# One hybrid attention and expert layer on one core: the router taken block by block, a ring of ten weight places, later rounds inside a pair, constant products in waits

## What is computed

```python
xp = xp + gt1 * _rmsnorm(out, g_post1[l])            # out = [conv, attention] @ w_out
h = _modulate(xp, g_pre2[l], sh2, sc2)               # rmsnorm(xp) * g * (1 + sc2) + sh2
xp = xp + gt2 * _rmsnorm(_hier_moe(h, *moe_w), g_post2[l])
...
def _hier_moe(h, w_rg, b_rg, w_re, b_re, w_gate, w_up, w_down):
    g_prob = jax.nn.softmax((xt @ w_rg) + b_rg, axis=-1)
    g_top, g_idx = lax.top_k(g_prob, 1)
    e_logits = ((xt @ w_re) + b_re).reshape(-1, N_GROUPS, E_PER_GROUP)
    e_sel = jnp.take_along_axis(e_logits, g_idx[:, :, None], axis=1)[:, 0]
    e_top, e_idx = lax.top_k(jax.nn.softmax(e_sel, axis=-1), TOP_K)
    ...
    for e in range(N_EXPERTS):                       # 32 experts
        he = jax.nn.silu(xt @ w_gate[e]) * (xt @ w_up[e])
        out = out + gates[:, e:e + 1] * (he @ w_down[e])
```

## Time and profile before

| | us |
|---|---|
| three runs: median, lowest, highest | 729.72, 726.66, 861.23 |
| the profiled execution, its own time | 726.36 |
| its span from first to last instruction | 724.6 |
| PE busy in the span | 589.2 (81%) |
| DVE, ACT, POOL busy | 258.9, 148.6, 84.8 |
| bytes moved, mean rate | 171.79 MB, 237 GB/s |

### The profile page before, as it was taken

The page is one execution under the profiler, slowest core; times in us unless marked ns, Lnnn a source line. Parts: engine busy times, 40 slices in busy tenths (PEclk is TensorE's granted clock), DMA queues, the critical chain, the costliest instruction groups (busy, mean ns, idle before and its releaser), DMA issues.

```text
span 724.6 us, 8142 instructions
## 1 busy us (share of the span) xinstructions
PE 589.2 (81%) x3118; PEld 308.6 (43%) x3119; DVE 258.9 (36%) x445; ACT 148.6 (21%) x298; POOL 84.8 (12%) x103
## 2 busy tenths in 40 slices
PE   0889899999999999989999348878998787778800
PEld 0656565655555455544455223333433233323400
DVE  2316899999442143312233540100110100000134
ACT  3220000012315444322223202100011000001233
POOL 5000000600000000001111035111111111110002
PEclk9999999999999999999999759989999999989965
DMA  9999926000008430044214921599999999999468
GB/s 334 344 374 383 357 89 231 14 0 1 0 1 326 176 145 1 1 152 196 117 58 185 395 71 31 197 413 410 424 424 425 425 426 426 425 426 428 202 268 187
DMA packets 49269, 171.79 MB, mean 237 GB/s; under 512 B 5722, under 2 KB 14267, under 8 KB 36938
## 3 DMA queue, kind: packets, MB, share of 16 engines
q1 hardware_dynamic: 41216, 156.11, 53.9%
q0 software_dynamic: 6736, 13.59, 6.1%
q10 hardware_dynamic: 1274, 1.52, 0.6%
HBM read 161.48 MB, written 17.06 MB: 246 GB/s over the span
## 4 chain that ended last, share of the span: by engine, by line
PE 60%; DMA 23%; DVE 5%; issue 3%; ACT 3%; PEldq 1%; PEld 1%; SPq 1%; DVEq 0%; ACTq 0%; POOLq 0%; POOL 0%
DMA arena<-in_w_up 14%; PE ps L1273 14%; PE ps L1457 10%; PE ps L1521 9%; DMA arena<-in_w_ada 6%; PE ps L1432 5%; PE ps L1534 4%; PE ps L1278 4%; PE ps L1274 4%; PE ps L1441 3%; PE ps L1291 2%; DMA arena<-h_d,idg 2%; PE ps L1357 2%; PE ps L1411 1%; ACT arena L870 1%
## 5 line engine op out<-in xcount | busy, mean ns | idle before, releaser
L1521 PE MATMUL ps<-arena 128*64 128x512 f32 x512 | 120.1, 622 | 22.1 <-DMA arena<-in_w_up 16.4
L1273 PE MATMUL ps<-arena 128*128 128x512 f32 x256 | 132.0, 597 | 1.2 <-issue 1.2
L998 DVE SCALAR_TENSOR_TENSOR arena<-arena 128x655 f32<-128x655 f32 x116 | 95.0, 897 | 0.4 <-issue 0.2
L1521 PEld LDWEIGHTS ps<-arena 128*64 128x64 f32 x512 | 44.8, 143 | 96.2 <-issue 92.2
L1278 PE MATMUL ps<-cst,arena 128*128 128x128 f32 (+2 forms) x349 | 54.0, 298 | 33.1 <-DVE arena L937 17.4
L1534 PE MATMUL ps<-arena 128*64 128x512 f32 x272 | 63.5, 609 | 16.3 <-ACT arena L870 15.8
L1274 PEld LDWEIGHTS ps<-arena 128*128 128x128 f32 x256 | 48.7, 190 | 61.5 <-issue 61.5
L1457 PE MATMUL ps<-arena 128*128 128x512 f32 x160 | 69.2, 593 | 0.9 <-ACT arena L822 0.9
L1278 PEld LDWEIGHTS ps<-cst,arena 128*128 128x128 f32 (+2 forms) x349 | 44.7, 178 | 50.8 <-issue 42.4
L1221 DVE TENSOR_TENSOR arena<-arena,ps 128x256 f32<-128x256 f32 x16 | 6.7, 421 | 129.6 <-ACT arena L875 117.2
L1274 PE MATMUL ps<-arena 128*128 128x128 f32 (+1 forms) x256 | 50.9, 280 | 0.0
(11 more groups left out here) (242 smaller groups left out, 519.9 us busy)
## 6 DMA issues: line engine op xcount, KB each, us to landing
arena<-in_w_gate SPq DMA_DIRECT2D x16, 2048.0 KB, 19.6
arena<-in_w_up SPq DMA_DIRECT2D x16, 2048.0 KB, 25.4
arena<-in_w_down SPq DMA_DIRECT2D x16, 2048.0 KB, 30.2
arena<-in_w_ada SPq DMA_DIRECT2D x12, 2048.0 KB, 13.8
arena<-y_d SPq DMA_DIRECT2D x10, 512.0 KB, 7.1
arena<-in_w_in SPq DMA_DIRECT2D x8, 512.0 KB, 12.3
arena<-in_w_out SPq DMA_DIRECT2D x1, 4096.0 KB, 12.6
arena<-ada_d SPq DMA_DIRECT2D x8, 512.0 KB, 10.1
```

Source lines behind the costliest of these rows:

```text
L998: ins = dve.scalar_tensor_tensor(dst, src, w, dst, ALU.mult, ALU.add)
L1273: mm(pp(name)[:, 0:TS], lhs(k), rhs_s(k), start=k == 0, stop=k == steps - 1)
L1521: last = mm(ps[a:a + ROWS, s, :], src[:, k, a:a + ROWS], slots[w][:, j, 0:2, k * FE:(k + 1) * FE], start=k == 0, stop=k == KD - 1)
```

## The change

Six things, all in the second half save for the last.

1. The router's choice is made for one block at a time, between the products of the next block's projection. PE turns x itself, not h2. The row a2 and the block's norm are folded in elsewhere: a2 is multiplied into the router's weights (`wr0` for the context, `wr` for the rest) by POOL, and b2 times the router's weights (`rb`) plus the bias becomes a row `biasrow`, spread over the partitions by two products (`small`) that DVE copies out. In `logits`, 128 tokens are now stationary and 36 columns move, so that nothing has to be turned back. `pos` and the tables' products are made for each block as well.
2. The last block is worked in two halves.
3. `keep_busy(n)` issues n products of constants (ones by identity, into bank 3) at three places after the last projection: 6, 14 and 12.
4. Weights lie in ten places of 2 MB (`pieces`): nine in `arena`, the tenth where blocks 0 to 3 of x lay. SP waits for each piece: gate and up places come free with `e_gu` (and `r_gu`), down places with `e_y`. Gate and up are separate products of 64x256 columns, each with its own wait. The pieces 5 and 8 (down of pairs 1 and 2) are loaded after the first gathers, piece 9 after x is stored.
5. Later rounds of a pair come between its gate and up products and its down product. The loops over pairs on SP and PE are written out. On POOL the order in pair 0 is now: more rows, gather for pair 2, the ten scatters, `later_ids`, later rounds, gather for pair 3, scatter of results.
6. In the first half PE gets four transposes (`turn34`) after q1 and eight products (`rb`) after `cache`. The router's weights are read from DRAM as rows `(k p)`, no longer `(p k)`.

```diff
-            act.dma_start(x_rg, i["w_rg"][0].rearrange("(p k) e -> p k e", k=KD)).then_inc(wr_in, 16)
+            act.dma_start(x_rg, i["w_rg"][0].rearrange("(k p) e -> p k e", p=P)).then_inc(wr_in, 16)
...
             landed(sp, f"P{NT - 1}")
-            load_pair(2, 2)
-            sp.wait_ge(h2_last, 1)
-            load_pair(1, 1, pieces=range(2, 3))
-            sp.wait_ge(x1_ready, NT)
+            for n in range(6, 8):
+                load(n)
+            sp.wait_ge(h2_ready, NT)
+            sp.wait_ge(x1_ready, NT + 1)
             sp.dma_start(out_rows(NT - 1), x[:, NT - 1, :]).then_inc(x_st, 16)
-
-            with sp.Fori(0, RINGS) as turn6:
-                for n in range(6):
-                    pair = 6 * turn6 + 3 + n
-                    sp.wait_ge(w_used, pair - 2)
-                    load_pair(pair, n % 3)
...
+            sp.wait_ge(xg_in[1], 16)
+            for n in (5, 8):
+                load(n)
+
+            sp.wait_ge(x_st, 16 * NT)
+            load(9)
+
+            sp.wait_ge(cnt_ready, 1)
+            for n in range(PLACES, 3 * PAIRS):
+                pair, kind = divmod(n - PLACES, 3)
+                if kind == 0:
+
+                    upto = sp.value_load(extra[0:1, PAIRS + pair + 1:PAIRS + pair + 2], min_val=0, max_val=PAIRS * (ROUNDS - 1))
+                    sp.wait_ge(e_gu, pair + 1)
+                    sp.wait_ge(r_gu, sp.snap(upto + 1))
+                elif kind == 2:
+                    sp.wait_ge(e_y, pair + 1)
+                load(n)
...
             dve.wait_ge(gg1_in, 32)
             dve.wait_ge(a2_in, 32)
             dve.wait_ge(b2_in, 32)
-            for name in POST:
...
+            dve.wait_ge(bias_in, 1)
+            dve.tensor_copy(biasrow, bias_ps).then_inc(bias_ready, 1)
...
+            begin(pe, "small")
+            pe.wait_ge(wr2_ready, 1)
+            for v in range(2):
+                last = mm(bias_ps[:, v, :], ones[0:G + E, :], diag[:, v, :], start=True, stop=True)
+            last.then_inc(bias_in, 1)
             pe.wait_ge(wo_in, 16)
-            pe.wait_ge(wr_ready, 1)
...
+            pe.wait_ge(bias_ready, 1)
+
+            def keep_busy(n):
+
+
+                for _ in range(n):
+                    mm(ps[:, 3, 0:P], ones[:], ident, start=True, stop=True)
...
+                for n, (k, half) in enumerate(steps):
+                    if b == 0 and k == 0:
+                        pe.wait_ge(mixc_ready, CM)
+                    if b and n == 6:
+                        turn_rows(b - 1)
+                    if b and n == 9:
+                        if b >= 2:
+                            pe.wait_ge(place_ready, b - 1)
+                        logits(b - 1)
+                    if b >= 2 and n == 12:
+                        table(0, b - 2)
+                    if b and n == 15:
+                        places(b - 1)
...
+                pe.wait_ge(e_xT, pair + 1)
+                gate_up(s, first, xT[:, s], e_gu)
+
+                with pe.If(n > 0):
...
+                        gate_up(1 - s, first, xT[:, 1 - s], r_gu)
...
-                pe.drain().then_inc(w_used, 1)
-
+                down(s, first + 2, heT[:, s], e_y)
```

More of the change, by code:

```diff
@@ L757, in _ @@
             act.drain().then_inc(cachekv_ready, 1)
+            landed(act, "rb")
+            free(act.activation(lgb[:], pp("rb")[0:G + E, 0:2], ACT.Identity, bias=rbias[:]), "rb")
             landed(act, "krdup")
@@ L1368, in _ @@
                 low_rank(n, name)
+                if n == 1:
+                    begin(pe, "turn34")
+                    pe.wait_ge(rows_ready, 5)
+                    for a in range(4):
+                        last = turn(pp("turn34")[:, a * P:(a + 1) * P], rows[:, 6 + a, :])
+                    done(last, "turn34")
             pe.wait_ge(sq_ready, QM)
@@ L1384, in _ @@
             done(last, "cache")
+            emptied(pe, "turn34")
+            pe.wait_ge(wr_ready, 1)
+            begin(pe, "rb")
+            for k in range(KD):
+                last = mm(pp("rb")[0:G + E, 0:2], wr[:, k, :], b2T[:, k, :], start=k == 0, stop=k == KD - 1)
+            done(last, "rb")
             emptied(pe, "kr")
@@ new lines, in _ @@
+            emptied(pe, f"P{NT - 2}")
+            keep_busy(6)
+            turn_rows(NT - 1)
+            pe.wait_ge(place_ready, NT - 1)
+            table(0, NT - 2)
+            logits(NT - 1)
+            keep_busy(14)
+            places(NT - 1)
+            pe.wait_ge(place_ready, NT)
+            table(0, NT - 1)
+            for a in range(NT):
+                for c in range(2):
+                    last = mm(cnt_ps, onesb[:], oh[:, c, a, :], start=a == c == 0, stop=a == NT - 1 and c == 1)
@@ L1496, in _ @@
+            last.then_inc(cnt_done, 1)
+            keep_busy(12)
+            pe.wait_ge(place_ready, NT + 1)
+            for b in range(NT):
+                table(1, b)
             for s in range(4):
-                n = sum(1 for name in order if place[name][0] == s)
+                n = homes.count(s) - (s == HOME["small"])
                 pe.wait_ge(drained[s], n)
```

646 lines of the change are left out of this document (339 added, 307 removed).

## The result

The changed kernel takes 724.4 us in the median of 18 runs (721.5 to 730.1), the kernel before 728.9. The ratio is 0.9944, with a 95% interval of 0.9925 to 0.9963: faster, but by 0.6%, where the forecast of 715 us meant 1.6 to 2%. The profiled execution has a span of 720.5 us, beside 724.6 before. So the direction and the range hold, and the size does not: against the forecast span of 714.0 the profiled execution is 6.5 us longer.

What follows compares the result with a forecast made beforehand. PE bounds up to the projections' end, the weight stream the experts. Projections end at 414.3, release at 456.1, last landing 674.8, PE's end 10.6 earlier: span 714.0, plus 1.8 is 715.8, given as 715; range 702 to 727.

Steps and rivals of the forecast that it cites:

- Part 1: Start to the end of the last projection (T): PE-path terms put it at 414.3, 23 later than before.
- the dearest line: PE's wait on bias_ready ahead of P0: P0 starts 7.7 later, bounds 5 to 9.
- 1 + 1.4 + 7.7 = 10.1: Delay of P0: router weights read as rows 1, turn34 and rb 1.4, the wait on bias_ready 7.7.
- The clock term of 2.3: PE's products behind the wait on bias_ready run at a lowered clock: 2.3 us lost, 0 to 4.
- 4.4 + 8.7 = 13.1: Router work inside the projections of blocks 1 to 4: turning x 4.4, 64 logits instructions 8.7.
- the estimate of 6.8: Alternative price of the 64 logits at the page's 107 ns a load, 1.9 less than the term used.
- Parts 2 and 3: Last projection to first expert product, T + 22.8, 15.4 shorter; then first release, pieces 10 and 11 at T + 41.8 = 456.1.
- Part 4: Weight stream from the release: 38 pieces at 5.73 plus 1, landing at 674.8; PE ends at 678.7, 10.6 earlier.
- two small gaps: In the stream, pieces 12 and 13 wait for pair 0's down and pair 1's gate and up products; 1 for both.
- The restart comes no earlier: POOL's ten scatters delay pair 3's gather, or block 4's store is slow: restart slides 4 to 8, 719 to 724; chance 0.29.
- PE falls to 1.2 GHz in the experts: PE stops at each piece and its clock drops; each such pair costs 10.6, three make 745; chance 0.08.
- The stalls of part 1 are smaller: Before the projections end, clock holds and loads overlap: 708, or 700 with the bias wait hidden; chance 0.18.

Runs made afterwards that it cites:

- the late bias wait: The change with PE's wait on bias_ready moved from ahead of P0 to ahead of block 0's logits; ratio 0.9912 to the kernel before.
- the gather first: The change with POOL's gather for pair 3 moved ahead of later_ids and the later round's scatter; ratio 0.9999 to the kernel before.
- the branch kernel: The change with the late bias wait, and scatter_ids and later_ids run only where some pair has a third round or more; ratio 0.9746, median 712.2 us.
- without the numbers: The change without the ten scatters of row numbers and their reading back (scatter_ids, later_ids); ratio 0.9882 to the kernel before.
- the branch but no constant products: The branch kernel without its three keep_busy calls; ratio 0.9819 to the kernel before.
- with twenty: Ten number scatters issued twice, the second ten into an unread table: on the change with the late bias wait, ratio 1.0057; on the kernel before, 1.0080.

## Why the prediction was right or wrong

**What bounds it.** Right: the end is the restart of the stream, plus the stream, plus a tail. In every kernel with the ring of ten the last down product waits for its weights. In the change PE ends at 685.7, 3.8 behind the last landing, where 3.9 was forecast.

**Part 1, T.** Forecast 414.3, measured 412.2. The wait on `bias_ready`, called the dearest line, is there:
```profile
327.71 2.90 PE L1604 MATMUL ps<-arena 128*128 128x512 f32 x3 [7.43 <-issue]
```
Its cue is DVE's copy of the bias row, which had waited 14.69 us for the transfers of a2 and b2:
```profile
327.37 0.23 DVE L1138 COPY cst<-ps 128x72 f32<-128x72 f32 x1 [14.69 <-DMA arena<-ada_d]
```
P0 starts 9.2 later than in the earlier trace rows; 1 + 1.4 + 7.7 = 10.1 was forecast. The clock term of 2.3 is 2.7 by the two groups shown. The router products were sized too high. From the chain in the change, one block's transposes and logits:
```profile
366.06 0.87 PE ps L1343 x8
366.94 2.58 PE ps L1604 x6
369.51 1.71 PE ps L1555 x16
```
If the four blocks are alike, they take 4 x (0.87 + 1.71) = 10.3 where 4.4 + 8.7 = 13.1 stood: 2.8 less, more than T's whole miss of 2.1. With the 0.9 less at P0 and the 0.4 more of the clock that makes 3.3 less, so 1.2 more lie somewhere else and were not placed. The nearest row in the trace of before had priced a load by a transposition at 136 ns; the logits took 1.71/16 = 107 ns. The Trainium skill (TensorE: Matmul & The Clock Gate, section LDWEIGHTS) has 107 ns for 128 columns; by that rule, the trace agrees, and the estimate of 6.8 for the 64 logits was the right one (6.84).

**Parts 2 and 3.** The first expert product at T + 22.8 forecast, T + 24.1 measured: close. Piece 10 at 456.1 forecast, at 454.1 measured, 42 behind T as put. This was partly luck. It holds only where no signal is held: with the late bias wait, with nine places, with the gather first and without the constant products piece 10 came some 52 behind T.

**Part 4 is the step that failed.** It said: 38 pieces at 5.73 and 1 for two small gaps, 218.7 us from the release to the last landing. It took 227.8. Two terms are behind that, the first of which stands in part 3.
- "Pieces 5, 8 and 9 start at T + 20.5 and fill what was the gap." They start there, and do not fill it. Piece 9 landed at 461.9, 7.8 behind the release, and 1.5 MB of these pieces had to be moved after it: at 409 GB/s that is 3.7 us. The forecast took the full rate for granted in a stretch with ten scatters in it, of which the earlier trace rows had told only that beside an empty queue they cost 2% of DMA.
- "[...] two small gaps. [...] so I take 1 for both: 674.8." Where everything had landed before the release (the branch kernel: from 446.66 to the last landing, 671.5), the stream still took 224.9, 6.2 more than 218.7. With the late bias wait, without the numbers, and with the branch but no constant products, where everything had landed as well, it took 224 to 226. The weight queue of the branch kernel moved 1.5 MB less in that time than the change's 82.21, which is the part of pieces 5, 8 and 9:
```profile
q1 hardware_dynamic: 10607, 80.69, 86.2%
```
  Here are its first stretches:
```profile
444.00:452.00 8.00, 6.59 (x44) 2.81 (x39) 0.42 (x1) 0.77 (x2) 0.00 (x0) 1.00 0.61 225
452.00:460.00 8.00, 6.84 (x46) 3.68 (x46) 2.45 (x2) 1.30 (x2) 1.21 (x2) 1.00 0.95 357
460.00:468.00 8.00, 6.98 (x62) 4.64 (x60) 0.42 (x1) 1.68 (x3) 2.02 (x2) 1.00 0.92 353
```
  The first release frees two places, 4.2 MB; one more comes 11.7 later and two after another 7.0 (the SP rows above). A ring of which PE frees single places starts with holes; before, three places came free at once. In the first 37.3 us of the stream the branch kernel moves 366 GB/s and the kernel before 397, which is 1.2 MB or 2.7 us. In the last 30 us it is 321 against 346, another 1.8 us. The rest was not taken apart. A gain in the restart is thus partly given back: 14.1 us earlier in the branch kernel (446.7 against 460.8), 12.7 earlier at the last landing, with one piece fewer to load, which should have been worth 5.7 more. The 3.7 and the 6.2 together are 9.9, near the 9.1 by which the change's stream was too long.

**The rivals.** "The restart comes no earlier" named the ten scatters and put 719 to 724 on it, with a chance of 0.29. It named the right place and the wrong path: it feared for POOL's own order (pair 3's gather, which came 8.8 later than before, at no cost to the stream), and the restart did not slide. The scatters acted on the stream's rate beside them and, in most variants, on PE's signals. That its time came true is luck. "PE falls to 1.2 GHz in the experts" did not happen: the granted clock is 1.00 from 440 to 480. It was low at the start of the first product (0.63 in 436 to 440) and behind the start of the gather's wait (0.51 in 490 to 500), as in the earlier trace rows, and no pair was slowed throughout. "The stalls of part 1 are smaller" did not happen: the wait and the clock behind it came as put, and only the router's products were cheaper.

**The chances.** Within 2% had 0.53, and within 2% it is. The sum's remaining account: T -2.1, the stage behind it +1.3, the release by part 3 -1.2, the stream +9.1, tail and end -0.6, together +6.5.

## What to carry over

Before counting a transfer as hidden in a gap of DMA, list what else moves into that gap; here ten scatters of a few kilobytes in all cost 4.5 us of the end, through the rate beside them and in some executions perhaps through late signals, where the kernel before had paid nothing for them. If small indirect DMAs serve a case that the data seldom has, put them under a branch: here that, with one wait moved behind work that needs nothing from it, made 0.6% into 2.5%. And a buffer that is freed piece by piece has a start-up cost of its own, so earlier loads are worth what the first releases can follow up, not their number.

## What the runs showed of the hardware

- PE's completion signals can reach the other engines 6 to 7 us late (8.5 and 19 us with twenty) while POOL issues a run of ten or more indirect DMAs of 128 x 4 bytes, reads or writes, whether or not the weight stream runs. PE itself goes on. With at most two under way it did not happen. In the kernel before it was 1.5 us with ten and nothing with twenty; why is open.
- DMA's busy share says nothing of its rate beside such traffic: in the change 0.99 at 182 GB/s in 448 to 456, 1.01 at 418 in the 8 us before.
- A product that waits 7.4 us for its cue pays for it again: the products behind it took 2.7 us more, with a granted clock of 0.50 (the 1.2 GHz level) in 326 to 332 and 0.90 in 332 to 338.
